# Second layer's gated scans: decay products built level by level, and covering units cut into banks between the levels

## The reference, cut to what matters

```python
def gla_chunk_scan(q, k, v, log_f):      # S_t = diag(f_t) S_{t-1} + k_t^T v_t ; o_t = q_t S_t
    ...
def hgrn2_mixer(cols, lb, o_gain):
    q, f, iv = cols[..., :w], cols[..., w:2*w], cols[..., 2*w:]
    log_f = logaddexp(log(lb), log1p(-lb) + log_sigmoid(f))
    k = (1.0 - lb) * sigmoid(-f)
    o = gla_chunk_scan(sh(q), sh(k), sh(iv), sh(log_f))      # 8 heads of 128
    return rms_norm(o, o_gain)
...
y = concat([mix, mem_out]) * silu(gate)
x = x + y @ w_out
```

## Time and profile before

| what | value |
|---|---|
| median of three runs | 1869.1 us |
| the profiled execution's own time | 1869.37 us |
| its span | 1867.6 us |
| mean granted TensorE clock | 0.997 |
| PE matmul busy | 1838.7 us, 98% of the span |
| DVE, ACT, POOL busy | 61%, 50%, 31% |
| first scan (`hg` 0), from its first cover to the end of `oscan` | 464.95 to 510.35 us |
| second scan (`hg` 1), from level 0 to the end of `oscan` | 546.25 to 585.04 us |

### The profile page before, as it was taken

How to read it: one execution, slowest core, us unless ns; L and a number is a source line. 1 busy time by engine, 2 the same in 40 slices (tenths; PEclk the granted TensorE clock), 3 DMA queues, 4 the chain that set the end, 5 groups by cost and what they waited for, 6 DMA issues and landing times.

```text
span 1867.6 us, 25503 instructions
## 1 busy us (share of the span) xinstructions
PE 1838.7 (98%) x10128; PEld 1587.1 (85%) x10128; DVE 1140.3 (61%) x2029; ACT 939.6 (50%) x1109; POOL 574.9 (31%) x128
## 2 busy tenths in 40 slices
PE   9999999999999999999999999999999999999998
PEld 7888887889887988888888888899888889888887
DVE  7887788886887886222867322567522287862227
ACT  7555555455554554444454544444444455544443
POOL 0000000000000004888001888300688700058880
PEclk9999999999999999999999999999999999999999
DMA  9434434544233336555543555545655543365551
GB/s 362 158 139 177 158 136 158 208 158 172 96 140 118 141 109 238 195 200 187 201 163 119 203 192 191 181 180 187 228 191 191 196 164 136 121 234 193 197 187 67
DMA packets 53049, 325.56 MB, mean 174 GB/s; under 512 B 8624, under 2 KB 11056, under 8 KB 15568
## 3 DMA queue, kind: packets, MB, share of 16 engines
q1 hardware_dynamic: 45328, 310.49, 45.5%
q10 hardware_dynamic: 7616, 13.59, 2.2%
HBM read 323.02 MB, written 1.05 MB: 174 GB/s over the span
## 4 chain that ended last, share of the span: by engine, by line
PE 85%; DVE 10%; issue 2%; ACT 2%; DMA 1%; SPq 1%; DVEq 0%; ACTq 0%
PE output L1104 31%; PE project L1104 30%; PE turn L1513 5%; PE project L1513 5%; PE project L1519 2%; PE turn L1519 2%; PE turn L1336 2%; DVE wlo L1988 2%; PE output L1301 1%; PE output L1276 1%; DMA raw<-in_units 1%; DVE arena L2328 1%; DVE arena L2105 1%; PE turn L1255 1%; DVE arena L2351 1%
## 5 line engine op out<-in xcount | busy, mean ns | idle before, releaser
L1063 POOL TENSOR_TENSOR wlo<-raw,whi 128x2048 fp32r<-128x2048 f32 x124 | 574.7, 4666 | 1244.2 <-ACT whi L1582 1227.5
L1582 ACT ACTIVATE whi<-raw 128x2048 fp32r<-128x2048 f32 x289 | 547.0, 1910 | 337.8 <-PE project L1513 166.2
L1104 PE MATMUL project<-whi,XT 128*128 128x512 f32 x1376 | 451.0, 398 | 1.9 <-ACT arena L1591 1.0
L1988 DVE TENSOR_TENSOR wlo<-raw,whi 128x2048 fp32r<-128x2048 f32 x165 | 375.0, 2285 | 22.1 <-ACT whi L1582 21.4
L1104 PEld LDWEIGHTS project<-whi,XT 128*128 128x128 f32 x1376 | 258.5, 188 | 56.5 <-DVE wlo L1988 1.3
L1104 PE MATMUL output<-whi,YTh 128*128 128x512 f32 x736 | 288.1, 391 | 1.5 <-DVE YTl L2478 1.5
L1104 PE MATMUL output<-whi,YTl 128*128 128x512 f32 x736 | 287.1, 390 | 0.0
L1104 PE MATMUL output<-wlo,YTh 128*128 128x512 f32 x736 | 286.9, 390 | 0.0
L2762 DVE TENSOR_TENSOR arena<-project,arena 128x256 f32<-128x256 f32 x48 | 20.4, 424 | 409.1 <-ACT arena L1944 409.1
L1104 PE MATMUL project<-wlo,XT 128*128 128x512 f32 x688 | 268.0, 390 | 0.0
L1104 PE MATMUL project<-XT,whi 128*128 128x256 f32 x1184 | 219.0, 285 | 0.0
(11 more groups left out here) (289 smaller groups left out, 2374.5 us busy)
## 6 DMA issues: line engine op xcount, KB each, us to landing
raw<-in_units SPq DMA_DIRECT2D x290, 1024.0 KB, 4.8
arena<-in_ln_g ACTq DMA_DIRECT2D x8, 512.0 KB, 5.5
arena<-in_ln_b ACTq DMA_DIRECT2D x8, 512.0 KB, 7.2
raw<-in_units SPq DMA_DIRECT2D x2, 512.0 KB, 7.4
tok<-in_mem SPq DMA_DIRECT2D x1, 1024.0 KB, 14.4
arena<-in_x_t SPq DMA_DIRECT2D x1, 1024.0 KB, 18.1
xres<-in_x SPq DMA_DIRECT2D x1, 1024.0 KB, 14.3
arena<-in_mem_t ACTq DMA_DIRECT2D x1, 1024.0 KB, 4.8
```

The source lines that it names most:

```text
L1063: pool.tensor_tensor(wlo[:, slot, :], raw[:, slot, :], whi[:, slot, :], ALU.subtract).then_inc(lo_pool, 1)
L1104: mm = pe.matmul(out, x if x_stationary else w, w if x_stationary else x, start=start and i == 0, stop=stop and i == 2, skip_group_check=True)
L1582: act.activation(whi[:, slot, :], raw[:, slot, :], ACT.Copy).then_inc(hi_done, 1)
L1988: dve.tensor_tensor(wlo[:, slot, :], raw[:, slot, :], whi[:, slot, :], ALU.subtract).then_inc(lo_dve, 1)
```

## The change

In the two scans of the first block, no logarithm, no cumulative sum and no Exp per level remains.

- `fgate`: ACT computes Exp, Ln and a second Exp (`RB`), all 128 x 1024. DVE multiplies once (128 x 1024), then makes k with four operations of 128 x 256, which release level 0, and the gates themselves with four more (`DB`). The Exp of part 1 is gone; the table load there stays.
- `z0`: DVE multiplies q by the gates (128 x 1024, releases level 1), then makes the products of the gates over blocks of 2, 4, ... 64 tokens (six operations on 512, 256, ... 16 columns), each waiting for the one before.
- Level l from 1 to 7: q and k of the next level are built from those of this level. The half of each block whose decay grows is multiplied by the block's product on DVE (two operations of 128 x 512, at level 7 of 128 x 256); the other half is copied as it is to the other buffer by ACT (`keep_halves`, same sizes). Both write the buffers that level l-1 read, so both wait for `lev_done` of that level; PE's level l+1 waits for both (`z_ready`, and the new semaphore `halves_kept`).
- Covering units are cut in two (`halved`): bank 0 ahead of one level, bank 1 ahead of the next. `hg` 0: halves ahead of levels 0, 1, 2, 3, 4, then two ahead of 5, one ahead of 6. `hg` 1: one half ahead of each of levels 1 to 6. Nothing stands ahead of levels 7 and 8.
- The two `turn`s of y stand ahead of level 0 instead of behind level 4; `hi` and `lo` of the units are put behind single levels.

```diff
+    def product_levels(hg, halves, pp=False, gq=None):
+        ...
+        for l in range(9):
+            for run in halves.get(l, ()):
+                run()
+            add("lev", kind="hgrn", hg=hg, l=l, L=L + l, ...)
+            if l == 8:
+                add("levend", kind="hgrn", hg=hg, L=L + 8, pp=pp)
+            for run in halves.get(l + 0.5, ()):
+                run()
+        n["L"] += 9
+        add("oscan", kind="hgrn", ...)
+
+    def halved(halves, l, run, at=(0, 1), scalar=0, vector=1):
+        ...
+        halves.setdefault(l + at[0], []).append(first)
+        halves.setdefault(l + at[1], []).append(lambda: kept[0]())
+        halves.setdefault(l + scalar + 0.5, []).append(lambda: add("ahead", n=kept[1], on="s"))
+        halves.setdefault(l + vector + 0.5, []).append(lambda: add("ahead", n=kept[1], on="v"))
...
-    c1[0]()
-    levels("hgrn", 0, c1[1:] + cover_of(wb, 3584, "gate", buf="y", gh=0)[1], [3, 8, 8],
-           turns=lambda: [turn("y", h, 2, "Y", 8) for h in range(H2)])
+    halved(halves, 0, lambda: one(0, halved=True))
+    halves[0].append(lambda: [turn("y", h, 2, "Y", 8) for h in range(H2)])
+    halved(halves, 2, lambda: one(1, halved=True))
+    halves[3.5].append(value_post)
+    halved(halves, 4, lambda: gate(0, halved=True))
+    halved(halves, 5, lambda: gate(1, halved=True), vector=2)
+    halves.setdefault(6.5, []).append(lambda: fields.append(gate_post(on="s")))
+    halves[7.5].append(lambda: add("post", on="v", **fields[0]))
+    product_levels(0, halves)
...
-    levels("hgrn", 1, [lambda: one(0, first=True), lambda: one(1), lambda: one(4)], [3, 5, 8], pp=True, gq=gq, ...)
+    halves = {0.5: [behind.pop(0)]}
+    halved(halves, 1, lambda: one(0, first=True, halved=True))
+    halved(halves, 3, lambda: one(1, halved=True))
+    halved(halves, 5, lambda: one(4, halved=True), vector=2)
+    halves[8.5] = [lambda: add("ahead", n=len(units), on="v")]
+    product_levels(1, halves, pp=True, gq=gq)
...
+        qPB, kPB = [ar(28, 1024), qFB], [kFB, ar(32, 1024)]
...
 # TensorE, step "lev"
                     if l or not g:
                         pe.wait_ge(z_ready, L + 1)
+                    if l >= 2 and not g:
+                        pe.wait_ge(halves_kept, 7 * (L // 9) + l - 1)
...
 # ScalarE
+            def keep_halves(l, L):
+                p = 1 - l % 2
+                act.wait_ge(z_ready, L + 1)
+                act.wait_ge(lev_done, L)
+                if l > 1:
+                    act.wait_ge(halves_kept, 7 * (L // 9) + l - 1)
+                act.activation(moved_halves(qPB[1 - p], l, 1, 0), moved_halves(qPB[p], l, 1, 0), ACT.Copy)
+                act.activation(moved_halves(kPB[1 - p], l, 0, 1), moved_halves(kPB[p], l, 0, 1), ACT.Copy)
...
 # ScalarE, step "fgate" part 0
-                    for j in range(4):
-                        ins = act.activation(x, x, ACT.Ln, bias=1.0, scale=lbs[:, c - 16 + 8:c - 15 + 8])
+                    act.activation(RB, kFB, ACT.Exp, scale=-1.0).then_inc(a2v, 1)
 # ScalarE, step "fgate" part 1
-                    act.wait_ge(v2a, nth("v2a"))
-                    act.activation(kFB, kFB, ACT.Exp).then_inc(a2v, 1)
 # ScalarE, step "lev" of these scans
+                    if 1 <= l < 8:
+                        keep_halves(l, L)
+                    if l:
+                        evacuate(f, l - 1, L - 1)
...
 # VectorE
+            def product_level(f):
+                l, L = f["l"], f["L"]
+                if 1 <= l < 8:
+                    p, d = 1 - l % 2, block_decays(l - 1)
+                    dve.wait_ge(lev_done, L)
+                    dve.wait_ge(z_ready, L + 1)
+                    if l > 1:
+                        dve.wait_ge(halves_kept, 7 * (L // 9) + l - 1)
+                    dve.tensor_tensor(moved_halves(qPB[1 - p], l, 1, 1), moved_halves(qPB[p], l, 1, 1), moved(d, l, 1, 0), ALU.mult)
+                    dve.tensor_tensor(moved_halves(kPB[1 - p], l, 0, 0), moved_halves(kPB[p], l, 0, 0), moved(d, l, 0, 1), ALU.mult)
+                if l:
+                    evacuate(f, l - 1, L - 1)
...
 # VectorE, step "fgate" part 0
-                    dve.tensor_tensor(DB, DB, kFB, ALU.subtract)
-                    dve.tensor_tensor(kFB, GB, kFB, ALU.subtract)
-                    scan(GB, DB)
+                    dve.tensor_tensor(GB, DB, RB, ALU.mult)
+                    for j in range(4):     # x: columns j*S to (j+1)*S
+                        ins = dve.tensor_scalar(kFB[:, x], GB[:, x], lbs[:, c:c + 1], None, ALU.mult)
+                    for j in range(4):
+                        dve.scalar_tensor_tensor(out=DB[:, x], in0=GB[:, x], scalar=lbs[:, c:c + 1], in1=RB[:, x],
+                                                 op0=ALU.mult, op1=ALU.add)
...
 # VectorE, step "z0"
-                    dve.tensor_copy(st[:, 92:93], st[:, 93:94]).then_inc(z_ready, 1)
-                    distances(False, 1)
+                    dve.tensor_tensor(qPB[0], qFB, DB, ALU.mult).then_inc(z_ready, 1)
+                    for l in range(1, 7):
+                        pairs = block_decays(l - 1).rearrange("p (n a) -> p n a", a=2)
+                        dve.tensor_tensor(block_decays(l), pairs[:, :, 0], pairs[:, :, 1], ALU.mult)
```

More of the change, by code:

```diff
@@ L145, in pieces, with one @@
         n["p"] += 1
-        def one(u, ahead=True, between=(), turned=False, split=None):
+        def one(u, ahead=True, between=(), turned=False, split=None, halved=False):
             f = dict(g=g, u=u, src=src, fm=feature_major, turned=turned, split=split)
+            if halved:
+                unit("proj", (w, "P", u, col), ahead=False, banks=(0,), **f)
+                m = len(units) - 1
+                return lambda: add("proj", n=m, ahead=False, banks=(1,), begin=False, **f)
             unit("proj", (w, "P", u, col), ahead=ahead, banks=(0,) if between else (0, 1), **f)
@@ L239, in begin_output, with one @@
         conv = w[0] == "conv_w_out"
-        def one(u, first=False, whole=False, scan=0, ahead=True):
-            unit("out", (w, "Q", u, 0), ahead=ahead, g=g, u=u, first=first, whole=whole, scan=scan, src=src, conv=conv, heads=len(heads))
+        def one(u, first=False, whole=False, scan=0, ahead=True, halved=False):
+            f = dict(g=g, u=u, first=first, whole=whole, scan=scan, src=src, conv=conv, heads=len(heads))
+            unit("out", (w, "Q", u, 0), ahead=not halved and ahead, hs=(0,) if halved else (0, 1), **f)
+            if halved:
+                m = len(units) - 1
+                return lambda: add("out", n=m, ahead=False, hs=(1,), begin=False, **f)
         def tail(u, *xs):
@@ L418, in plan, with levels @@
     quad("mem", vg, par=2, g=3)
-    def levels(kind, hg, cover, lag_to, pp=False, gq=None, turns=None, ahead_of_scan=None):
+    def levels(kind, hg, cover, lag_to):
         L = n["L"]
         every = 9 / (len(cover) + 1)
-        at = [int((i + 1) * every) - (kind == "hgrn") for i in range(len(cover))]
+        at = [int((i + 1) * every) for i in range(len(cover))]
         gates = n["pd"]
@@ L434, in levels @@
             hold[0] = False
-            add("lev", kind=kind, hg=hg, l=l, L=L + l, heads=len(heads), gq=gates if gq is None else gq, gates=gates, pp=pp, t=n["t"])
+            add("lev", kind=kind, hg=hg, l=l, L=L + l, heads=len(heads), gq=gates, gates=gates, pp=False, t=n["t"])
             if l == 8:
-                add("levend", kind=kind, hg=hg, L=L + 8, pp=pp)
+                add("levend", kind=kind, hg=hg, L=L + 8, pp=False)
             release()
-            if turns is not None and l == 4:
-                turns()
             for x in [x for x in lags if x[0] <= l]:
@@ L1228, in output_unit @@
                     pe.wait_ge(q_evac, g4)
-                for h in range(H2):
+                for h in hs:
                     for c in range(2):
@@ L1403, in _ @@
                     qf, kf = (qFG, kFG) if g else (qFB, kFB)
-                    if l:
-                        qf = QE[l % 2] if g else ZB[l % 2]
-                        kf = KE[l % 2] if g and l < 7 else qf
+                    if l and not g:
+                        qf, kf = qPB[1 - l % 2], kPB[1 - l % 2]
+                    elif l:
+                        qf = QE[l % 2]
+                        kf = KE[l % 2] if l < 7 else qf
                     for j in range(4):
```

145 lines of the change are left out of this document (86 added, 59 removed).

## The result

The changed kernel takes **1858.5 us** (median of 4 runs, 1858.07 to 1860.02). The kernel before, timed beside it, takes 1870.01 (4 runs, 1868.71 to 1871.97). The ratio is 0.9939 [0.9928, 0.9951]: 11.5 us are gone. The forecast was 1858.6. Run once more, in the last group of experiments, the changed kernel took 1859.95, ratio 0.9944 [0.9931, 0.9956]: two medians of one kernel can differ by 1.4 us. The profiled execution took 1858.07 us, its span is 1855.9, so 11.7 us less than the 1867.6 before.

A forecast was written before the change was run, and what follows sets the result against it. PE was taken as the bound, busy 1838.7 of 1867.6 us, so only its waits and slow clock could be won: 12.32 us, less 0.5, 1.0, 0.1 and 0.2, gives 10.5, so 1858.6 us (own range 1856.5 to 1861; wider 1856 to 1864).

The forecast's parts named there:

- Idle in the scans: PE's waits in the two scans, 4.22 + 3.11 = 7.33 us; all to go except about 0.5 before each level 8.
- `fgate`: PE's wait at the second scan's `fgate` for a bank ACT must empty: 0.77 us becomes 0.1.
- Clock: Level 8, second scan's level 7 and first part of `oscan` at low clock: 4.22 us to come back.
- The reason I gave for its staying: Clock should stay over a 0.5 us wait, since the trace had 1.00 over 1.40 us between large matmuls.
- less activity can bring the clock down: Clock rival: clock still falls near level 7, levels 6 and 7 back to back; 4.2 us stay, 1862.8; chance 0.15.
- Returns from a level to a unit: Halved cover adds three returns in each scan at 0.08 us: 0.5 us lost on PE.
- Later: Behind the second scan, DVE's backlog could start the norm late: 0.2 us lost.
- Sum: Total gain: 12.32 - 0.5 - 1.0 - 0.1 - 0.2 = 10.5 us.
- level 8's wait: Before level 8, about 0.5 us stays in each scan behind ACT's copies and score move; 1.0 for both.
- the tail rival: Levels 7 and 8 wait 2 us again and the clock falls: gain 2.8, 1866.3 us; chance 0.07.

The follow-up runs named there:

- the last group of experiments: Changed kernel with a half unit kept for level 8 (1857.52 us), score move shared (1858.71), or both (1859.83), beside the unchanged changed kernel.
- Whole units: Changed kernel with covering units whole again at their old places, products and turns kept; 1862.73 us, ratio 0.9965 to the kernel before.
- turns late: Changed kernel with the two turns of y behind level 4 again; 1857.93 us, ratio 0.994 to the kernel before.
- one more Exp: Changed kernel with the gate stage's last Exp done twice on ACT in both scans; 1860.05 us, ratio 0.994 to the kernel before.
- move shared: Changed kernel with the move of level 6's lower scores given from ACT to DVE; 1858.71 us, ratio 0.9934 to the kernel before.
- products doubled: Changed kernel with two further DVE products in each level below 7, four operations for two; 1860.46 us, ratio 0.9933 to the kernel before.
- before's arithmetic at the new places: Kernel before with its logarithms, sums and per-level Exp, but units cut and placed and turns moved as changed; 1877.99 us, ratio 1.0036.
- the two kernels with the wait put in: Changed kernel with DVE products repeated to make PE wait 3.0 us ahead of level 7 (1866.48 us) or level 8 (1866.76 us).

## Why the prediction was right

Point by point:

- *Idle in the scans*: 7.33 us were to fall to 1.0; they fell to 1.10. Every wait but level 8's is gone, and that one is 0.55 us for the cause forecast. By the Trainium skill (ScalarE: Activation LUTs, "What ACT_TABLE_LOAD costs") the copy of 256 columns was to take 0.40 and the wait to be 0.55; the trace has 0.42 and 0.40, and 0.55. My own 0.37 and 0.5 lay a little under. What ends the wait is, as forecast, ACT's move of level 6's scores behind its two copies.
- *`fgate`*: 0.77 was to become 0.1; the gap is 0.13.
- *Clock*: 4.22 us were to come back, and the windows read 1.00. That it had cost that much fits the traces: at full clock level 7 to the end of `oscan` takes 4.70 us, and it took 6.25 (510.35 - 503.53, less the wait of 0.57) and 7.37 (585.04 - 577.67) before, 4.2 us more. That the long wait brings the fall is shown by the waits put back in. The reason I gave for its staying, that the trace held 1.00 over a wait of 1.40 us between large matmuls, was no rule, as the last section shows. That wait also stands behind eight transposes of 128x128, not behind a large matmul, and its row reads 1.46. The rule of the Trainium skill (TensorE: Matmul & The Clock Gate, "What's actually happening") that less activity can bring the clock down had a chance of 0.15. Levels 6 and 7 did close up, and the clock did not fall there in this profile.
- *Returns from a level to a unit*: **the one term that was mis-sized.** I took 0.5 us off. Busy time in the two scans at full clock was 41.18 + 35.68 - 4.22 = 72.64 us before; it is 39.06 + 32.71 = 71.77 after, 0.87 less where I had 0.5 more. Whole units give 39.15 + 32.58 = 71.73 by the same cut, so the halves cost nothing: a pair of levels takes 491.50 - 488.01 = 3.49 us from its start to the unit's, two levels apart 474.84 - 473.14 = 1.70 each, and the 0.09 so saved pays the 0.08 of the return. The 0.87 comes with the waits. A pair with a wait of 0.24 in its middle took 3.97 us before, from its start to what follows it, 3.73 without the wait itself, against 3.49 run through:

```profile
488.54 1.89 PE L1416 MATMUL output<-arena 128*128 128x64 f32 x16
490.68 2.00 PE L1416 MATMUL output<-arena 128*128 128x64 f32 x16 [0.24 <-DVE arena L2334]
492.51 1.04 PE L1336 MATMUL turn<-ident,arena 128*128 128x128 f32 x8
```

Four such pairs stood in the two scans, with waits of 0.43, 0.24, 0.78 and 0.23; without the wait they took 3.69, 3.73, 3.69 and 3.71, so 0.20 to 0.24 us more than run through, 0.86 in all. A wait there costs that much more than the idle time shown.
- *Later*: 0.2 was to be lost behind the second scan; from its end to the next wait's end is 8.48 us (581.60 - 573.12), and was 8.38: 0.1.
- *Sum*: 10.5 + 1.37 (this term) - 0.1 (level 8's wait) + 0.1 (later) = 11.9. The stretches give 5.79 + 0.64 + 5.53 = 11.96, less the 0.1 behind. The profiled executions differ by 11.3 and the medians by 11.5, within the runs' spread of 2 us. That the forecast lies 0.1 from the median measured is in part luck: the gain forecast was 10.5, counted from 1869.1, and beside the changed kernel the one before read 0.9 higher.

The other durations: `lbs` times gates plus `RB` took 1.67 us (1.3 forecast) and the block products 2.17 (1.8); both end well ahead of their need. Products with the repeated operand read 0.68 and 0.69, as forecast; those of 128x256 read 0.42, not 0.29, which ACT's longer work covers. Two slips in the rivals change nothing: the tail rival's own terms give a gain of 2.6, not 2.8, and the slowest 128x512 operation of DVE in the rows is the score move with 1.29, not 1.26.

What the prediction did not see is how the parts hang together. By their ratios the products and the turns without the halves win 0.35%, some 6.5 us, the new places alone lose 0.36%, some 7 us, and both together win 0.61%. It credited both with taking the waits away and did not price either alone. When I then priced the places alone in the expectation, only the wait at level 0 was right (2.7, measured 2.77). I left out the way over ACT ahead of level 7, `lo` and the post ahead of level 8, and the clock, which with such waits stays low in both tails: level 8 took 2.07 us in the first scan and 1.88 in the second.

## What to carry to other kernels

Look first at what a hand-off passes through: here a step that goes DVE, ACT, DVE still waited with half a unit of cover (0.98 and 1.50 us at the worst middle level of the two scans) and 2.3 us with none, while in the kernel after two parallel operations waited for nothing with half a unit and 0.55 us at most with none. So shorten the chain first, and only then cut the cover and spread it. Where a wait between small matmuls goes, expect slightly more than its shown length back (0.20 to 0.24 us here), and the slow matmuls behind it if the clock fell there. When a level waits, look also for the bank that it reuses, and compare the end of the named releaser with what the program waits for.

## What the hardware showed that was not expected

Behind the second scan PE waits 1.46 us for the norm, behind a few transposes; the wait is there in all 14 profiled executions. In the kernel after, the clock stays. The windows of PE behind that wait (581.60):

```profile
582.00:583.00 1.00, 1.00 (x6) 1.00 0.26 23
583.00:585.00 2.00, 2.00 (x10) 1.00 0.47 111
```

And with the turns late, where the scans are as long, the wait is the same 1.46 us and ends at 581.72:

```profile
582.00:583.00 1.00, 1.00 (x4) 0.54 0.36 51
583.00:585.00 2.00, 2.00 (x7) 0.50 0.56 101
```

It fell to its 1.2 GHz level in 4 of the 14 profiled executions (turns late, one more Exp, move shared, products doubled) and stayed in 10. The same kernel seems to have it both ways: the mean granted clock of the five executions of turns late reads 0.998, 1.000, 0.998, 1.000 and 0.999, and the first is the one profiled. Turns late spans 1857.5 us where the kernel after spans 1855.9, with the same waits in the scans. Together with the wait of 3.00 us that once kept the clock and once lost it, this says that a wait gives the fall a chance and not a verdict; what decides it these runs leave open. In the tails, levels 6 to 8 and `oscan`, the longer waits went with it: where the longest wait was 2.0 to 3.5 us it fell in 9 of 10 (before twice, before's arithmetic at the new places, and the two kernels with the wait put in), and where it was 1.49 us or less in none of 18.
